# Two transformer blocks on one core: the start's rounding through banks, the post norms' sums earlier, and constant products in two waits

## The reference, cut to what matters

```
for l in range(2):
    h = rmsnorm(x, g_pre_mix[l])
    p = h @ w_in[l]              # and four branches: attention, pooling, gated mixing, convolution
    merged = gate0 * y_a + gate1 * y_b + gate2 * y_c + gate3 * y_d
    x = x + rmsnorm(merged @ w_out[l], g_post_mix[l])
    h = rmsnorm(x, g_pre_ffn[l])
    f = (silu(h @ w_ffn_gate[l]) * (h @ w_ffn_up[l])) @ w_ffn_down[l]
    x = x + rmsnorm(f, g_post_ffn[l])
# second block: modulation from c_2, neighbourhood attention, gated linear attention, a SwiGLU FFN
rmsnorm(x, g) = x * rsqrt(mean(x * x) + 1e-6) * g
```

## Time and profile before

| | us |
|---|---|
| median of three runs | 2561.21 |
| the profiled execution, its own time | 2561.25 |
| its span, first to last instruction | 2559.5 |
| TensorE busy | 2511.0 |
| GpSimd busy | 1784.3 |
| VectorE busy | 1134.1 |
| ScalarE busy | 582.9 |

### The profile page before, as it was taken

How to read it: one execution, slowest core, us unless ns; L and a number is a source line. 1 busy time by engine, 2 the same in 40 slices (tenths; PEclk the granted TensorE clock), 3 DMA queues, 4 the chain that set the end, 5 groups by cost and what they waited for, 6 DMA issues and landing times.

```text
span 2559.5 us, 33853 instructions
## 1 busy us (share of the span) xinstructions
PE 2511.0 (98%) x11930; PEld 2039.0 (80%) x11930; DVE 1134.1 (44%) x1656; ACT 582.9 (23%) x1000; POOL 1784.3 (70%) x816
## 2 busy tenths in 40 slices
PE   8999999999999999999999999989999999899999
PEld 6878787788888787878778888868888788688887
DVE  7764423644454756442364445455227732311100
ACT  3233312311111224231231110032323520211100
POOL 6766678588888576667768888725352467588887
PEclk9999999999999999999999999989998999999999
DMA  4222223233355232222323336511122223233343
GB/s 141 91 83 82 86 90 96 66 98 98 113 208 181 66 91 82 82 90 91 97 67 92 96 123 207 198 31 50 50 67 83 67 82 97 68 98 95 93 119 102
DMA packets 70202, 250.74 MB, mean 98 GB/s; under 512 B 8304, under 2 KB 8432, under 8 KB 70000
## 3 DMA queue, kind: packets, MB, share of 16 engines
q1 hardware_dynamic: 66816, 241.74, 30.3%
q10 hardware_dynamic: 3312, 7.95, 0.9%
HBM read 247.56 MB, written 2.10 MB: 98 GB/s over the span
## 4 chain that ended last, share of the span: by engine, by line
PE 67%; issue 11%; POOL 11%; DMA 9%; DVE 2%; ACT 0%; SPq 0%; POOLq 0%; DVEq 0%; ACTq 0%
PE bank L479 16%; PE bank L475 16%; PE bank L476 16%; DMA w_raw<-weights 8%; POOL w_lo L401 6%; POOL w_hi L398 5%; PE bank L429 3%; PE bank L431 3%; PE bank L430 3%; PE bank L740 1%; PE bank L1105 1%; PE bank L749 1%; PE bank L1089 1%; PE bank L765 1%; PE bank L1079 1%
## 5 line engine op out<-in xcount | busy, mean ns | idle before, releaser
L398 POOL TENSOR_TENSOR w_hi<-w_raw,one 128x1024 fp32r<-128x1024 f32 x405 | 776.8, 1918 | 734.5 <-PE bank L479 445.7
L401 POOL TENSOR_TENSOR w_lo<-w_raw,w_hi 128x1024 fp32r<-128x1024 f32 x405 | 1009.1, 2492 | 31.8
L475 PE MATMUL bank<-act_hi,w_hi 128*128 128x512 f32 x1808 | 713.9, 395 | 2.9 <-POOL w_hi L398 2.6
L476 PE MATMUL bank<-act_lo,w_hi 128*128 128x512 f32 x1808 | 704.8, 390 | 0.0
L479 PE MATMUL bank<-act_hi,w_lo 128*128 128x512 f32 x1872 | 464.3, 389 | 0.0
L479 PEld LDWEIGHTS bank<-act_hi,w_lo 128*128 128x128 f32 x1872 | 350.9, 188 | 73.5 <-issue 1.0
L475 PEld LDWEIGHTS bank<-act_hi,w_hi 128*128 128x128 f32 x1808 | 340.0, 188 | 81.1 <-issue 9.4
L476 PEld LDWEIGHTS bank<-act_lo,w_hi 128*128 128x128 f32 x1808 | 340.1, 188 | 73.4 <-issue 3.8
L475 PE MATMUL bank<-f_hi,w_hi 128*128 128x512 f32 x528 | 205.4, 389 | 0.0
L476 PE MATMUL bank<-f_lo,w_hi 128*128 128x512 f32 x528 | 205.4, 389 | 0.0
L479 PE MATMUL bank<-f_hi,w_lo 128*128 128x512 f32 x528 | 131.4, 389 | 0.0
(11 more groups left out here) (435 smaller groups left out, 3494.8 us busy)
## 6 DMA issues: line engine op xcount, KB each, us to landing
w_raw<-weights SPq DMA_DIRECT2D x405, 512.0 KB, 3.6
mod_raw<-mods SPq DMA_DIRECT2D x48, 512.0 KB, 4.4
bias<-bias ACTq DMA_DIRECT2D x8, 512.0 KB, 4.6
resid<-x SPq DMA_DIRECT2D x8, 256.0 KB, 5.4
out<-resid ACTq DMA_DIRECT2D x8, 256.0 KB, 4.6
params<-params ACTq DMA_DIRECT2D x2, 534.5 KB, 3.6
ctx_raw<-ctx SPq DMA_DIRECT2D x1, 1024.0 KB, 4.8
second<-second SPq DMA_DIRECT2D x1, 972.5 KB, 6.9
```

Of the source, the lines that this page charges most:

```text
L398: nc.gpsimd.tensor_tensor(w_hi[:, j, :], w_raw[:, j, :], one[:, 0:1].to_broadcast([P, 1024]), ALU.mult)\
L401: nc.gpsimd.tensor_tensor(w_lo[:, j, :], w_raw[:, j, :], w_hi[:, j, :].bitcast(F32), ALU.subtract).then_inc(blocks_split, 1)
L475: mm(out, w_hi[:, slot, tile * P:tile * P + P], rows_hi, start=start, stop=False)
L476: mm(out, w_hi[:, slot, tile * P:tile * P + P], rows_lo, start=False, stop=False)
```

## The change

1. **Start.** ScalarE squares tiles 0, 2, 4, 6 and 7 (SQUARED_BY_ACT), VectorE tiles 1, 3 and 5. For tiles 4 to 7 ScalarE first writes x times gain to a free bank (2 to 5), waits for itself (x_in_bank) and rounds from the bank to raw_hi; VectorE takes the bank minus raw_hi as raw_lo.
2. **First sums.** y_norm_sums is cut in two. y_norm_first (identity and the sums over seven tiles) stands inside the last output tile, between its high and its low products; y_norm_last stands where both were. For this the loop over the two halves of down is written out (in all three FFNs).
3. **Constant products.** keep_warm(n) multiplies ones by a constant 128 x 512 into bank 5, n times, which nobody reads: two ahead of the spread behind w_out, three behind it.
4. **Copies.** VectorE's wait for ScalarE's four copies to y stands behind y_norm and not ahead of it.
5. **Order of VectorE.** In add_rows, where a low part follows (both w_out norms and layer 0's FFN norm), tile k is added, then tile k+1 is scaled, then tile k's low part is made. It was: scale k+1, add k, low part of k-1.

```diff
+SQUARED_BY_ACT = (0, 2, 4, 6, 7)
...
-            def y_norm_sums(n):
+            def y_norm_first(n):
                 nc.tensor.transpose(bank[7][:, P:2 * P], ident, ident).then_inc(ident_placed, 1)
                 pe.wait_ge(y_sum, 8 * n + 7 + 2)
                 for tt in range(TT):
                     mm(bank[7][:, 0:4], sum_sq[:, tt * P:tt * P + P], pick[:, 3 - tt:7 - tt], start=(tt == 0),
                        stop=False)
+            def y_norm_last(n):
                 pe.wait_ge(y_sq, 8 * n + 8)
...
+            def keep_warm(n):
+                for _ in range(n):
+                    mm(bank[5][:, :], ones, rope, start=True, stop=True)
...
             def block_product(... , norm=None):
                     high_parts(out, slot, t, rows_hi[:, k, :], rows_lo[:, k, :], start and t == 0)
+                if norm is not None:
+                    y_norm_first(norm)
                 take(b)
...
-                with pe.Fori(0, 2) as i:
+                for i in range(2):
...
-                y_norm_sums(2 * l)
+                y_norm_last(2 * l)
+                keep_warm(2)
                 y_norm_spread(2 * l)
+                keep_warm(3)
...
-                if k % 2 == 0:
+                if k in SQUARED_BY_ACT:
                     run(tmp[:, k % 4, :], resid[:, k, :], ACT.Square).then_inc(x_sq, 1)
-                raw_high(0, k)
+                if k < 4:
+                    raw_high(0, k)
+                elif k > 4:
+                    run(bank[k - 3][:, :], resid[:, k - 1, :], ACT.Copy, scale=g_pre[:, k - 1:k]).then_inc(x_in_bank, 1)
+                    act.wait_ge(x_in_bank, k - 4)
+                    run(raw_hi[:, k - 1, :], bank[k - 3][:, :], ACT.Copy).then_inc(raw_hi_ready, 1)
...
-                    following = scaled(k + 1) if k < KT - 1 else None
+                    following = scaled(k + 1) if k < KT - 1 and then is None else None
                     dve.wait_ge(step.sem, there)
                     v.tensor_tensor(resid[:, k, :], resid[:, k, :], tmp[:, k % 4, :], ALU.add).then_inc(x_ready, 1)
+                    if then is not None:
+                        following = scaled(k + 1) if k < KT - 1 else None
+                        then(k)
...
-            for j in (KT - 2, KT - 1):
-                raw_low(0, j)
+            for k in range(4, KT):
+                dve.wait_ge(raw_hi_ready, k + 1)
+                v.tensor_tensor(raw_lo[:, k, :], bank[k - 2][:, :], raw_hi[:, k, :].bitcast(F32), ALU.subtract)
...
+                y_norm(2 * l)
                 for m in range(4):
                     dve.wait_ge(bank_free[m], use("out", m, 0, l) + 3)
-                y_norm(2 * l)
```

40 lines of the change are left out of this document (22 added, 18 removed).

## The result

| | kernel before | changed kernel |
|---|---|---|
| median, lowest, highest of its runs, us | 2561.21, 2560.36, 2562.98 (6 runs) | 2546.80, 2542.78, 2554.37 (6 runs) |
| profiled execution, span | 2561.25, 2559.5 | 2543.32, 2541.5 |
| mean granted clock of the span | 0.981 | 0.989 |

The ratio is 0.9947, with a 95% interval of 0.9929 to 0.9964: faster by 14.4 us in the median, where 6.8 were forecast. The sign was right; the time lies 7.6 us under the forecast and 4.4 under the range. Note the spread. The six runs of before lie within 2.6 us, those of the changed kernel within 11.6, and its profile is one of its fastest. So a comparison of two profiles does not explain the median here, and I use several.

What follows compares the result with a forecast made beforehand. TensorE, busy 98% of the span, was taken as the bound, losing time only to waits and low clock. The terms -3.5 - 5.3 + 0.7 + 1.3 = -6.8 us gave 2554.4 us, range 2551.2 to 2559.5.

Steps and rivals of the forecast that it cites:

- Start, -3.5: At the start, block 2 begins 1.95 us earlier and runs 1.54 us shorter at full clock: -3.5 us.
- Rival C: The start gives only 1.5 us because ScalarE, with five operations more, sets raw_hi later: 2556.4 us, 10%.
- First sums, a loss of 1.1 per place: Four post norms: sums moved ahead of the low products are no longer hidden in TensorE's wait, 1.1 us later.
- Copies, 0.66 per place: Same four places: VectorE's reciprocal no longer waits for ScalarE's copy of the last tile, 0.66 us back.
- Mix norms, -2.65 each: Behind w_out, both layers: first FFN tile 1.3 us earlier, second 1.3 us more at full clock; -2.65 us per layer.
- rival A: Mix norms: the 1.6 us hole drops the clock, constant products restore it; 1.6 us saved per layer, 2556.5 us, 15%.
- D: Mix norms: clock falls before 445.7 us, constant products run at half clock; +3.1 us per layer, 2565.9 us, 5%.
- FFN norm, layer 0, +0.7: Layer 0's FFN norm: spread's product starts 0.66 us later, VectorE's new order gives nothing; +0.7 us.
- FFN norm, layer 1, +1.3: Layer 1's FFN norm: VectorE's first add loses 0.1 us ahead of GpSimd's split or 2.5 behind; middle, +1.3 us.
- rival B: Layer 1's FFN norm: GpSimd's split goes before VectorE's add, 1.2 us more than forecast, 2555.6 us, 12%.
- The range's lower end: Whole kernel: 2551.2 us, with hand-overs free, add first, and a half-clock stretch less in an FFN norm.
- free hand-overs: At the start, ScalarE's hand-overs to itself (up to 0.1 us each) cost nothing; the start then saves 4 us.

Runs made afterwards that it cites:

- e2: The changed kernel without its five constant products behind each w_out; median 2559.27 us, ratio to the kernel before 0.9989.
- e15: The changed kernel unaltered, a third profile of the same program, one run; 2551.75 us.
- e3: The changed kernel with the first sums put back behind the last low product in all four places; median 2548.66 us, ratio to before 0.9943.
- e1: The kernel before with the change of the start alone; median 2559.77 us, ratio 0.9993.
- e10: The kernel before with only VectorE's wait for the copies moved behind y_norm, in both norms; median 2553.43 us, ratio 0.9965.
- e5: The kernel before with only the five constant products in the mix norms (two ahead of the spread, three behind); median 2548.36 us, ratio 0.9948.
- e11: The changed kernel with first sums back, wide products in FFN norms and second block, two low parts later at the start; median 2542.20 us, ratio to before 0.9928.
- e14: The changed kernel unaltered, a second profile of the same program, one run; 2547.97 us.
- e4: The kernel before with three constant products (2.6 us) ahead of the second weight block, nothing else; median 2565.31 us, ratio 1.0013.
- e16: The kernel before with only the copies waited for later, unaltered second profile of that program, one run; 2548.37 us.
- e7: The changed kernel with two wide constant products among the second block's narrow gated linear attention products; median 2543.76 us, ratio to before 0.9936.
- e9: The kernel before with two wide constant products among the second block's narrow gated linear attention products, nothing else; median 2558.45 us, ratio 0.9991.
- e8: The changed kernel with wide constant products also in the feed-forward post norms (one behind sums, three behind spread); median 2546.88 us, ratio to before 0.9943.
- e6: The changed kernel with three constant products (2.6 us) added ahead of the second weight block; median 2552.89 us, ratio to before 0.9961.
- e13: The kernel before with only the three constant products behind the spread in the mix norms; median 2554.92 us, ratio 0.9967.

## Why the prediction was wrong, step by step

- **Start, -3.5.** The profile gives -4.1, by the named rows. The clock stayed full through the second block, as assumed. What was missed is the second form: e2 has -1.6, e15 -0.2, e3 +1.5, and the whole start alone moved the median by only 1.2 us (e1). Rival C allowed for a loss of 2.0 us here; in four of nine starts 2.5 us and more were lost, for another reason than its own: not ScalarE's operations, but raw_lo beside GpSimd's split, and in three of them a half-clock stretch at about 55 us.
- **First sums, a loss of 1.1 per place.** Right: 1.0 in each mix norm (e3 against the changed kernel), with the standing wait of 0.7 to 0.8 us where it was said to be.
- **Copies, 0.66 per place.** The reciprocal stands right behind the root. Alone at half clock it gives 0.5 (e10), at full clock 1.3: e3's 3.9 less e5's 2.6, with VectorE's new order in it.
- **Mix norms, -2.65 each.** Right: -2.9 and -3.0. The first tile came 1.34 us earlier against its surroundings (5.47, less the 4.13 that the kernel was ahead); the forecast was 1.3. The clock held, in all six traces of kernels with constants and the sums moved, and in e3, e5 and e11 with the sums behind. None of these traces shows rival A or D.
- **FFN norm, layer 0, +0.7.** Measured +0.7.
- **FFN norm, layer 1, +1.3.** This step failed: -2.6, and -4.2 and -4.1 in the other two traces. Up to the first of the eight tiles its size was met, by luck: that tile came 1.27 us later (1650.57 us, against 1660.28 less the 10.98 that the kernel was ahead). VectorE's add did go first, so rival B did not come true. For this case the step wrote 0.1 us, but by its own terms the 0.66 us by which the spread's product comes later are lost all the same. The product came 1.17 us later and not 0.66, since the one-column products ahead of it took 2.39 us instead of 1.70, the end of them at half clock, and the add took 1.34 instead of 1.22. What the step had wrong is what follows: it took for granted that the stretch at half clock would last. The timeline of the changed kernel, then the same products in the kernel before:

```profile
1648.52 1.34 DVE L1697 TENSOR_TENSOR resid<-resid,tmp 128x512 f32<-128x512 f32 x1
...
1650.57 2.08 PE L476 MATMUL bank<-spread,const 128*128 128x512 f32 x2 [0.64 <-ACT spread L1235]
...
1655.91 1.80 PE L476 MATMUL bank<-spread,const 128*128 128x512 f32 x2
...
1657.91 1.10 PE L476 MATMUL bank<-spread,const 128*128 128x512 f32 x2
```

```profile
1660.28 2.08 PE L466 MATMUL bank<-spread,const 128*128 128x512 f32 x2 [0.52 <-ACT spread L1219]
...
1673.31 1.92 PE L466 MATMUL bank<-spread,const 128*128 128x512 f32 x2
...
1675.42 1.10 PE L466 MATMUL bank<-spread,const 128*128 128x512 f32 x2
```

  At half clock a tile takes 2.56 to 2.76 us in this loop, at full clock 1.31. Here three of the eight ran at half clock, the third in part; in the kernel before there were six. From the first to the eighth tile it is 12.56 us instead of 16.45, and these 3.9 us are what the forecast lacks. The range's lower end allowed for one stretch less in such a norm, with the 1.5 us that are left when free hand-overs (0.5) and the add first (1.2) are taken off its 3.2.
- **What the sum had no term for.** -1.6 at 883 us, -6.3 at 1934 and +1.6 at 1801 us. They were in the trace of before as half-clock stretches, and I took them as fixed, because no line of the change is near them. Steps for the first profile: -4.1 -2.9 +0.7 -1.6 -3.0 -2.6 +1.6 -6.3, and +0.3 at the end, -17.9. With the forecast's terms for the same places it was -6.8.

Which step explains the median, and not only the first profile? Of the three traced runs of the changed kernel e14 (2547.97 us) lies nearest to the median of 2546.80. Its row sums to -13.3, 6.5 us more than forecast, and layer 1's feed-forward norm is 5.5 of them; 883 and 1934 us give nothing there. In e15 it is 5.4, and the slow start takes 3.3 back. So the failed step is that of the feed-forward norm of layer 1, and behind it the assumption that stretches at half clock keep their length. The 6.3 us at 1934 us belong to some runs only, among them the first profile.

Why should a stretch depend on edits hundreds of microseconds away? e4's row suggests a reason, which is not shown. Its distance to the 2.88 us by which its falls came later was 0.57 us behind the start, then 0.29, 0.14, 0.08 and 0.01: but for the stretch at 883 us, which left it as it was, each one took away about half of it or more. So in this pair of traces the program drew into step with its half-clock stretches. The kernel before has such stretches behind w_out in both layers. It may therefore arrive at the later ones in nearly the same position each time and meet the half clock at 883, 1655 and 1934 us; that would fit its runs, 70 of 76 within 3.5 us. The constant products take the stretches behind w_out away, and the program would then arrive at the later ones in a position that changes from run to run.

Two things stand against this or beside it. e10 keeps both stretches behind w_out whole (10.24 us each), and still its runs go over 7.1 us, and both its traces leave the one at 1655 us after 6.83 us. And e1 is no evidence for it: its trace still has 3.85 of the 4.0 us of its start at the last block, with the falls behind the start 3.84 us earlier.

What is shown is that one and the same program has a stretch in some runs and not in others (e14, e15, e16), and that the clock held at 1934 us in all three traces with wide products there (e7, e9, e11) and fell in 13 of the 15 without. The two that kept it, the first profile of the changed kernel and e5, are also the only two of these 15 whose stretch at 1801 us lasted 6.83 us and not 3.41. In layer 0's feed-forward norm wide products removed the stretch in e8 and left 3.41 of its 13.65 us in e11. For layer 1's feed-forward norm the traces show one more link: in the seven where the spread's product ended ahead of the fall (e3, e6, e10, e13 to e16) the stretch lasted 6.83 us, or 13.65 (e3 and e13); in the nine others without wide products there it lasted 13.65 to 20.48. So where the program stands when the clock falls goes together with how long the stretch lasts. That the position alone decides is an inference; no run here sets it alone.

## What to carry to other kernels

A stretch at half clock is a cost that any edit upstream can move: list the granted clock over the whole span, give each stretch a price, and put those prices into the range, in both directions. Waits of a few microseconds and runs of narrow products can be worth filling with wide ones whose result nobody reads; here both waits had to be filled (medians: all five 2548.36 us, the three behind the spread 2554.92, the two ahead of it 2560.62). Where nothing waits, as at 1934 us, the price of 1.3 us must be set against the 6.2 that only some runs lose. When single runs of a kernel spread by far more than those of its predecessor, one pair of profiles explains neither median, and two more traces of the same program tell more than another variant.

## What was not expected of the hardware

- Busy and wide are two things for the clock: TensorE busy for 14.00 of 14.00 us had a granted clock of 0.51 (before, 1934 us; products of 64 and 128 columns up to 1944.5 us, wider ones behind them), and 1.00 over the same stretch once two products of 512 and 256 columns stood among them (e9). Without them it was 1.00 there in two of 15 traces.
- The same program on the same data had a stretch of 13.65 us at half clock at 1921.03 us (e14) and at 1924.85 us (e15), and none there in its first profile, with 6.2 us between them.
- A lag of 2.31 us grew to 2.87 us over five stretches at half clock without any change of the work, where the falls of the clock came 2.88 us later (e4, one pair of traces).
- Two raw_lo operations took 1.41 us ahead of GpSimd's first split and 3.04 us beside it; with one operand in a bank, 0.69 us each in both cases.
